# Output projections two tiles side by side, the pool mixer in fp32 ahead of the attention, gate chunks in the norms' tails

## The chip, the cores and the metric

The kernel runs on one core of a Trainium2 chip. A core has five engines with queues of their own: TensorE (PE, matmuls), VectorE (DVE), ScalarE (ACT), GpSimd (POOL) and SyncE (SP, which here issues the loads and stores). They work on SBUF, an on-chip memory of 128 partitions; PE writes to PSUM, 8 banks of 512 fp32 columns by 128 partitions. Each engine takes its instructions in order and waits on semaphores. The metric is the device time of one execution in microseconds.

## The reference

One inference step of a backbone of two layers over 1152 tokens (128 context tokens and 1024 latent tokens), width 1024, all in fp32:

```python
for l in range(DEPTH):                       # DEPTH = 2
    ada = silu(cond) @ w_ada[l] + b_ada[l]
    sh1, sc1, g1, sh2, sc2, g2 = split(ada, 6)
    u = layer_norm(x) * (1 + sc1) + sh1
    m = even_mixer(u) if l == 0 else odd_mixer(u)
    x = layer_norm(ALPHA * x + g1 * (m @ w_out[l]), ln_g[l, 0], ln_b[l, 0])
    u = layer_norm(x) * (1 + sc2) + sh2
    f = conv_ffn(u)                          # (silu(conv3(u @ w_up_a)) * (u @ w_up_g)) @ w_down
    x = layer_norm(ALPHA * x + g2 * f, ln_g[l, 1], ln_b[l, 1])

def even_mixer(u):    # layer 0
    q, k, v, p = split(u @ w_in)             # 512, 128, 128, 512 columns
    attn = attention(rope(rms(q)), rope(rms(k)), v)      # 8 heads, 2 key heads
    for g, w in enumerate((2, 4, 8, 16)):    # four groups of 128 columns
        pool[g] = (centred_mean(p[g], w) - p[g]) @ w_pool[g] * pool_scale[g]
    return concat(attn, pool)

def odd_mixer(u):     # layer 1
    h, b, c, f = split(u @ w_in)             # 768, 768, 768, 256 columns
    return concat(b * conv3(c * h), fourier(f))
```

`cond` is one vector for the latent and one for the context tokens; shifts, scales and gates follow from it. The new keys and values of the context are outputs too.

## The kernel before

The program is written out engine by engine; nothing schedules it, so the order of each engine's instructions is the order of its block of code, and semaphores tie the engines together.

**Products.** Nearly every fp32 product is made of three passes in fp32r, a reduced format: each operand is split into a rounded high part and the rest, the low part, and high*high, high*low and low*high are added in PSUM (`PASSES`). ACT rounds (`copy`, L812) and DVE subtracts (`lo`, L1272); of the weights of layer 0's output projection, four k-blocks are cast on DVE (L1502) and subtracted on POOL (`out_split`, L757). A few small products run in plain fp32: gates (L1795), columns for shift and scale (L1772, L1773, L1783), transposes (L1805).

**Tiles.** Tokens are taken as 9 tiles of 128 (the first is the context) or 3 chunks of 384. The contraction over 1024 columns is 8 k-blocks of 128. `act_a` and `act_b` hold activations transposed, k-block by k-block, high and low; the first four k-blocks of `act_b` are the attention's output, the last four the pool mixer's. In layer 1 the first six k-blocks of `act_a` are the conv mixer's and two the Fourier mixer's.

**Start.** SP issues the loads of constants, small parameters and bias rows, then w_ada in pieces of 512 KB into six slots. PE transposes the parameters into columns (L1741), ACT applies silu to the conditioning (L817), PE multiplies it with w_ada (L1751), and `top_cols` turns the first four blocks into columns: for two vectors and 8 k-blocks one matmul on the ada row (L1772) and one on the bias row (L1773), both in plain fp32.

**Layer 0.** POOL computes the pooled means in `pp`; PE, ACT and DVE make q, k and v. The attention goes over 18 groups (9 tiles x 2 key heads): `peak_scores` (L1937) and DVE's maxima (L1437), scores (L1958), exp on ACT (L1014), rounding on ACT, POOL's `p_low` (L749), the weighted sum (L1973, L1980), and DVE's division (L1442, L1448). When it is over, the pooled values are split into `ph` (ACT, DVE), mixed (L2033), scaled into `mf` on ACT (L1082) and split again into `act_b`, in turn with the weights `wo`.

**`ln_mid`.** In both layers it makes the output projection and the norms. `gates` expands three of four gate rows (g2 and g1, each for latent and context) over the partitions into banks 6 and 7, and ACT copies each. `project(tile)` makes 2 halves x 8 k-blocks x 3 passes = 48 matmuls of 512 columns into banks 2 x (tile mod 3) and the next. Then `ln_turn(tile)` (transposes of the second norm's output) alternates with `project(tile + 3)`, and in the tail with the three chunks of the first up unit of the feed-forward stage. The norm's chain for one tile is: DVE multiplies by the gate out of PSUM (L1324), adds alpha x (L1327) and takes statistics; ACT takes the root and normalises (L898); POOL applies gain and bias (L768, L770); DVE statistics again; ACT normalises into `ln_z` (L918); PE transposes (L1805); ACT modulates (L887) and rounds; DVE subtracts. `ln_act` and `ln_vec` run it in steps: in step s, ACT modulates tile s-2 first, then normalises tile s, then makes `ln_z` of tile s-1, and DVE takes up tile s, then s-1, then s-2. SP stores each normed tile, loads the next residual tile, and behind the last store issues the down weights' loads, the accumulator's loads (1.5 MB each) and the third up unit's.

**Feed-forward.** Eleven rounds in each layer, two up units and two gate units of 3 chunks in each, then the down projection (L2060) over 9 tiles, added up on DVE (L1556). A chunk is 24 matmuls (L1848).

## Time and profile before

| | us |
|---|---|
| runs, median (lowest to highest) | 3004.55 (3000.55 to 3005.01) |
| the profiled execution's own time | 3004.68 |
| its span, first to last instruction | 3002.9 |
| PE busy | 2771.1 |
| DVE busy | 1556.7 |
| ACT busy | 938.5 |
| POOL busy | 419.4 |

The profile is of one execution. Its times run from the span's start. The granted clock is the share of full speed that TensorE's clock had, 1.0 for 2.4 GHz and 0.5 for 1.2 GHz. In a timeline a row is one or several like instructions: start, duration, engine, line, tiles written and read, count, and in brackets the engine's idle time before it with what ended it. PEld is the weight load that goes with each matmul, SPq and ACTq are DMA issues. A plain fp32 matmul shows as two records.

### The profile page before, as it was taken

The page shows a single profiled execution, that of the slowest core. Times are in us where ns is not written, and L with a number is a line of the kernel's source. Part 1 is how long each engine was busy: PE and PEld are TensorE (multiplying, and loading weights), DVE is VectorE, ACT ScalarE, POOL GpSimd, SP SyncE. Part 2 cuts the span into 40 slices and gives each one's busy share as a digit, 9 for nine tenths or more (in the row PEclk, how much of TensorE's full clock was granted, in tenths as well). Part 3 has the DMA queues.
Part 4 walks back from the last instruction along what each step waited for, and adds up shares of the span by engine and source line. Part 5 has one row for each costly group of instructions (what it writes and reads, how often), then busy time and mean ns, then how long its engine had stood idle before and what let it go on. Part 6 is the DMA issues. An engine that isn't in the chain of part 4 may idle for free.

```text
span 3002.9 us, 36504 instructions
## 1 busy us (share of the span) xinstructions
PE 2771.1 (92%) x13992; PEld 2444.7 (81%) x13992; DVE 1556.7 (52%) x2166; ACT 938.5 (31%) x1417; POOL 419.4 (14%) x222
## 2 busy tenths in 40 slices
PE   6698699779899999999997899989899999999997
PEld 2387577648899999999993789968899999999996
DVE  0326688736555555555556333335655555555557
ACT  1611477635422222222224421124522222222223
POOL 0023377524000000000007000003200000000002
PEclk8799799979999999999998899989999999999999
DMA  7710100022311111111118131221311111111112
GB/s 288 265 46 7 42 1 1 0 77 86 134 43 42 42 42 42 42 42 42 42 36 288 56 103 38 69 85 64 145 40 40 42 42 42 42 42 42 42 35 77
DMA packets 172260, 202.26 MB, mean 67 GB/s; under 512 B 6843, under 2 KB 125207, under 8 KB 172179
## 3 DMA queue, kind: packets, MB, share of 16 engines
q1 hardware_dynamic: 171859, 200.83, 20.1%
q8 instruction: 54, 0.88, 0.1%
q10 hardware_dynamic: 320, 0.33, 0.0%
q14 instruction: 27, 0.22, 0.0%
HBM read 181.80 MB, written 19.33 MB: 67 GB/s over the span
## 4 chain that ended last, share of the span: by engine, by line
PE 79%; DVE 7%; ACT 5%; DMA 4%; POOL 3%; issue 2%; SPq 1%; ACTq 0%; POOLq 0%; DVEq 0%
PE ps L1848 47%; PE ps L2060 17%; PE ps L1826 7%; POOL p_low L749 2%; DVE small L1437 2%; DMA late_w<-in_w_ada 1%; DMA ada_w<-in_w_ada 1%; PE ps L1980 1%; PE ps L1795 1%; ACT p_top L812 1%; ACT p_exp L1014 1%; PE ps L1896 1%; ACT ln_u L887 1%; DMA raw_d<-in_k_pos 1%; PE ps L1937 1%
## 5 line engine op out<-in xcount | busy, mean ns | idle before, releaser
L1848 PE MATMUL ps<-act_b,uw 128*128 128x384 f32 x4608 | 822.2, 340 | 11.0 <-DVE act_b L1272 7.3
L1848 PEld LDWEIGHTS ps<-act_b,uw 128*128 128x128 f32 x4608 | 818.8, 189 | 12.9 <-DVE act_b L1272 7.9
L1848 PE MATMUL ps<-act_a,uw 128*128 128x384 f32 x3456 | 617.6, 340 | 5.3 <-DVE act_a L1272 5.3
L1848 PEld LDWEIGHTS ps<-act_a,uw 128*128 128x128 f32 x3456 | 614.5, 190 | 7.3 <-DVE act_a L1272 5.6
L2060 PE MATMUL ps<-dw,hh 128*128 128x512 f32 x2112 | 502.9, 397 | 8.7 <-DVE acc L1556 8.6
L2060 PEld LDWEIGHTS ps<-dw,hh 128*128 128x128 f32 x2112 | 398.1, 189 | 115.0 <-DVE acc L1556 10.4
L1556 DVE TENSOR_TENSOR acc<-acc,ps 128x512 f32<-128x512 f32 x360 | 246.8, 688 | 229.9 <-PE ps L2060 229.9
L812 ACT ACTIVATE fa<-ps 128x384 f32<-128x384 f32 (+2 forms) x176 | 67.5, 411 | 856.4 <-PE ps L1848 856.4
L1517 DVE TENSOR_SCALAR ft<-fa,fgrp 128x1153 f32<-128x1153 f32 x44 | 38.8, 883 | 309.9 <-ACT fa L812 309.9
L1272 DVE TENSOR_TENSOR uw<-raw_u,uw 128x1024 fp32r<-128x1024 f32 x112 | 136.7, 1222 | 117.5 <-ACT uw L812 113.8
L749 POOL TENSOR_TENSOR p_low<-p_exp,p_top 128x1536 fp32r<-128x1536 f32 (+1 forms) x50 | 170.9, 3418 | 92.1 <-ACT p_top L812 92.1
L1584 DVE TENSOR_TENSOR fh<-ft,ps 128x384 f32<-128x384 f32 (+2 forms) x176 | 75.2, 452 | 181.4 <-PE ps L1848 173.6
L812 ACT ACTIVATE uw<-raw_u 128x1024 fp32r<-128x1024 f32 x112 | 117.8, 1052 | 80.8 <-PE ps L1848 67.4
L794 POOL TENSOR_TENSOR acc<-acc,gb_end 128x1024 f32<-128x1024 f32 x9 | 21.4, 2378 | 835.3 <-ACT acc L1150 835.3
L812 ACT ACTIVATE hh<-fh 128x384 fp32r<-128x384 f32 x132 | 66.5, 520 | 218.7 <-DVE fh L1584 218.7
L787 POOL TENSOR_SCALAR acc<-acc,stats 128x1024 f32<-128x1024 f32 x9 | 10.8, 1202 | 832.7 <-DVE stats L1308 832.7
L1437 DVE TENSOR_REDUCE small<-ps 128x1 f32<-128x1152 f32 (+1 forms) x72 | 89.1, 1238 | 41.9 <-PE ps L1937 41.2
L768 POOL TENSOR_TENSOR ln_y<-ln_y,gbm 128x1024 f32<-128x1024 f32 x18 | 43.3, 2403 | 478.1 <-ACT ln_y L898 478.1
L1826 PE MATMUL ps<-wo,act_b 128*128 128x512 f32 x432 | 102.9, 399 | 0.0
L1826 PE MATMUL ps<-wo,act_a 128*128 128x512 f32 x432 | 102.3, 397 | 0.0
L887 ACT ACTIVATE ln_u<-ps,cols 128x128 f32<-128x128 f32 x216 | 78.4, 468 | 71.6 <-PE ps L1805 60.8
L1826 PEld LDWEIGHTS ps<-wo,act_b 128*128 128x128 f32 x432 | 82.6, 193 | 19.4 <-issue 2.3
(201 smaller groups left out, 3158.1 us busy)
## 6 DMA issues: line engine op xcount, KB each, us to landing
raw_u<-in_w_up SPq DMA_DIRECT2D x88, 512.0 KB, 3.7
ada_w<-in_w_ada SPq DMA_DIRECT2D x64, 512.0 KB, 6.4
raw_d<-in_w_down SPq DMA_DIRECT2D x44, 512.0 KB, 3.5
late_w<-in_w_ada SPq DMA_DIRECT2D x32, 512.0 KB, 6.0
raw_u<-in_w_in_odd SPq DMA_DIRECT2D x20, 512.0 KB, 3.6
ln_y<-in_x_all SPq DMA_DIRECT2D x18, 512.0 KB, 4.3
xs<-ln_y SPq DMA_DIRECT2D x18, 512.0 KB, 2.6
acc<-xs SPq DMA_DIRECT2D x6, 1536.0 KB, 11.5
```

What stands on the lines that cost most here:

```text
L749: gp.tensor_tensor(p_low[:, s % 3, 0:nb, :], p_exp[:, s % 2, 0:nb, :], p_top[:, s % 3, 0:nb, :].bitcast(F32), ALU.subtract).then_inc(p_lo, 1)
L768: gp.tensor_tensor(y, y, gb[:, 0, :], ALU.mult).then_inc(g_mul, 1)
L812: return act.activation(o, i, ACT.Copy)
L887: o = act.activation(ln_u[:, k * P:(k + 1) * P], ps[:, 6 + k // 4, (k % 4) * P:(k % 4 + 1) * P], ACT.Identity, bias=cols[:, l, c0, k, cc:c ...
L1272: return v.tensor_tensor(dst, src, hi.bitcast(F32), ALU.subtract)
L1437: v.tensor_reduce(g.peak(h), ps[:, 0:nb, 0:nw], mybir.AxisListType.XY, ALU.max, negate=True).then_inc(mx_done, 1)
L1517: chain(v.tensor_scalar(dst[:, 1:1 + n], line[:, 0:n], w(0), w(3), ALU.mult, ALU.add))
L1556: return v.tensor_tensor(a, a, ps[:, 6 + j % 2, :], ALU.add).then_inc(down_added, 1)
L1584: o = v.tensor_tensor(f_h[l][:, s0:s0 + ln], f_t[l][:, p0:p0 + ln], ps[:, 3 + c, s0 - c * CH:s0 - c * CH + ln], ALU.mult)
L1826: mm = pe.matmul(ps[:, 2 * (tile % 3) + h, :], src[:, k, a, tile * P:(tile + 1) * P], wo[l][:, k, w, 512 * h:512 * (h + 1)], start=(k, a, ...
L1848: mm = pe.matmul(out, uw[:, u_slot, w, k, :], src[:, k, a, c * CH:(c + 1) * CH], start=(k, w, a) == (0, 0, 0), stop=(k, w, a) == (KD - 1, ...
L2060: mm = pe.matmul(ps[:, 6 + h, :], hh[l][:, b, a, tile * P:(tile + 1) * P], w_[:, b, w, 512 * h:512 * (h + 1)], start=(b, a, w) == (0, 0, 0 ...
```

## The change

**Start.** The constants and eight of the small loads move from SP's queue to ACT's; SP issues three small loads (conditioning, context conditioning, and the first 2048 values of `b_ada` as 16 more rows of the matrix that is transposed anyway) ahead of w_ada. The bias thereby becomes 16 columns of `par`. `top_cols` has one matmul for each k-block, and DVE adds the bias when it copies the columns out (`cols_of`).

**Pool mixer.** w_pool stays fp32, `ph` and its splitting go. Twelve pieces of 384 tokens are multiplied in plain fp32: three ahead of the last keys' transpose, one ahead of the first peak scores, eight between the four peak scores of group 0. ACT scales them into `mixed`. They are split behind the attention.

**Splitting of `wo` in layer 0.** ACT rounds all eight k-blocks, DVE subtracts all eight; `out_split` on POOL is gone. The order is 7, 6, 2, 3, 5, 4, 0, 1, and the splits of `mixed` and those of the last attention group stand among them. SP loads gate rows, residual tiles and gains earlier.

**`ln_mid`.** Tiles 0 and 1 are projected side by side, the contraction outermost, so that each k-block waits only for itself; the four gates stand between k-blocks, g1 first. The other projections run one tile further ahead of the transposes. In the tail, chunks of the first up unit and of the first gate unit alternate, and both units are split before the norms.

```diff
             def top_cols():
-                pe.wait_ge(b_top, 32)
                 pe.wait_ge(ada_bank, 3 + ADA_TOP)
                 for n in range(2):
                     for k in range(KD):
-                        out = ps[:, 6 + n, 2 * k:2 * k + 2]
-                        pe.matmul(out, ada_top[:, 2 * n + k // 4, (k % 4) * P:(k % 4 + 1) * P], con[:, C_FOLD:C_FOLD + 2], start=True, stop=False)
-                        mm = pe.matmul(out, bias_row[n][0:1, k * P:(k + 1) * P], con[0:1, C_SELB:C_SELB + 1].broadcast_to([1, 2]), start=False, stop=True)
+                        mm = pe.matmul(ps[:, 6 + n, 2 * k:2 * k + 2], ada_top[:, 2 * n + k // 4, (k % 4) * P:(k % 4 + 1) * P],
+                                       con[:, C_FOLD:C_FOLD + 2], start=True, stop=True)
...
+            def mix(m):
+                g, c = divmod(m, NCH)
+                bank = MIX_BANKS[m % 3]
+                if m == 0:
+                    pe.wait_ge(pool_done, 1)
+                    pe.wait_ge(wp_ld, 16)
+                    pe.wait_ge(qkv_free, NT - 1)
+                if m >= 3:
+                    pe.wait_ge(mix_ev, m - 2)
+                for u0, ln, p0 in PPIECES[c]:
+                    mm = pe.matmul(ps[:, bank, u0 - c * CH:u0 - c * CH + ln], wp[:, g, :], pp[:, g, p0:p0 + ln], start=True, stop=True)
+                mm.then_inc(mix_done, 1)
...
             turn_queries(0)
+            mix(3)
             for h in range(G):
                 peak_scores(0, h)
+                mix(4 + 2 * h)
+                mix(5 + 2 * h)
...
-                gates(l)
-                project(0)
-                pe.wait_ge(gate_rdy, 4 * l + 3)
-                gate(0, ln_u)
-                project(1)
-                project(2)
-                pe.wait_ge(gate_rdy, 4 * l + 4)
-                for tile in range(NT):
-                    ln_turn(tile, i4)
-                    if tile + 3 < NT:
-                        project(tile + 3)
-                    if tile >= NT - 3:
-                        first_chunk(tile - (NT - 3))
+                gate_after = {2: 1, 4: 2, 5: 3, 6: 4} if l == 0 else {-1: 1, 4: 2, 5: 3, 6: 4}
+                def side_by_side():
+                    if -1 in gate_after:
+                        mid_gate(l, gate_after[-1])
+                    for n, k in enumerate(OUT_ORDER):
+                        ready(k)
+                        for tile in range(SIDE):
+                            for h in range(2):
+                                for a, w in PASSES:
+                                    mm = pe.matmul(ps[:, 2 * tile + h, :], src[:, k, a, tile * P:(tile + 1) * P], wo[l][:, k, w, 512 * h:512 * (h + 1)],
+                                                   start=n == 0 and (a, w) == (0, 0), stop=n == KD - 1 and (a, w) == (1, 0))
+                            if n == KD - 1:
+                                mm.then_inc(out_done, 1)
+                        if n in gate_after:
+                            mid_gate(l, gate_after[n])
+                side_by_side()
+                for tile in range(SIDE, 4):
+                    project(tile)
+                pe.wait_ge(gate_rdy, 4 * l + 4)
+                for tile in range(5):
+                    ln_turn(tile, i4)
+                    project(tile + 4)
+                for tile, c, gate_unit in ((5, 0, 0), (6, 0, 1), (7, 1, 0), (8, 1, 1)):
+                    ln_turn(tile, i4)
+                    first_chunk(gate_unit, c)
+                first_chunk(0, 2)
+                first_chunk(1, 2)
```

The order of PE's instructions in layer 0, from the attention's end to the first transposes of the norms, before (L2033 the mixer, L1795 gates, L1826 projections, L1805 transposes):

```order
L1980 MATMUL ps<-p_low,vv 128x512 x3
L2033 MATMUL ps<-ph,wp 128x384 x36
L1795 MATMUL ps<-ln_z,con 128x512 x4
L1795 MATMUL ps<-ln_u,con 128x512 x2
L1826 MATMUL ps<-wo_110,act_b 128x512 x48
L1795 MATMUL ps<-ln_u,con 128x512 x2
L1826 MATMUL ps<-wo_110,act_b 128x512 x96
L1805 MATMUL ps<-con,ln_z 128x128 x8
```

and now (L1864 the two tiles side by side, L1816 gates, L1879 single tiles, L1826 transposes):

```order
L2053 MATMUL ps<-p_low,vv 128x512 x3
L1864 MATMUL ps<-wo_112,act_b 128x512 x36
L1816 MATMUL ps<-ln_u,con 128x512 x2
L1864 MATMUL ps<-wo_112,act_b 128x512 x24
L1816 MATMUL ps<-ln_u,con 128x512 x2
L1864 MATMUL ps<-wo_112,act_b 128x512 x12
L1816 MATMUL ps<-ln_z,con 128x512 x2
L1864 MATMUL ps<-wo_112,act_b 128x512 x12
L1816 MATMUL ps<-ln_z,con 128x512 x2
L1864 MATMUL ps<-wo_112,act_b 128x512 x12
L1879 MATMUL ps<-wo_112,act_b 128x512 x96
L1826 MATMUL ps<-con,ln_z 128x128 x8
```

The mixer has left this place, the first gate stands behind three k-blocks, and two more single tiles come before the first transposes.

PE at the tail of layer 0's norms, before (the last projection, then transposes and chunks of the up projection):

```order
L1826 MATMUL ps<-wo_110,act_b 128x512 x48
L1805 MATMUL ps<-con,ln_z 128x128 x8
L1848 MATMUL ps<-act_b,uw 128x384 x24
L1805 MATMUL ps<-con,ln_z 128x128 x8
L1848 MATMUL ps<-act_b,uw 128x384 x24
L1805 MATMUL ps<-con,ln_z 128x128 x8
L1848 MATMUL ps<-act_b,uw 128x384 x240
```

and now:

```order
L1879 MATMUL ps<-wo_112,act_b 128x512 x48
L1826 MATMUL ps<-con,ln_z 128x128 x8
L1905 MATMUL ps<-act_b,uw 128x384 x24
L1826 MATMUL ps<-con,ln_z 128x128 x8
L1905 MATMUL ps<-act_b,uw 128x384 x24
L1826 MATMUL ps<-con,ln_z 128x128 x8
L1905 MATMUL ps<-act_b,uw 128x384 x24
L1826 MATMUL ps<-con,ln_z 128x128 x8
L1905 MATMUL ps<-act_b,uw 128x384 x216
```

Four transposes instead of three stand behind the last projection, and three chunks among them instead of two.

DVE behind the attention of layer 0, now (`mixed` is the mixer's output, `wo` from `raw_d` k-blocks 7, 6, 0, 1 and from `out_raw` 2, 3, 5, 4):

```order
L1293 TENSOR_TENSOR act_b<-mixed_100,act_b 128x1152
L1293 TENSOR_TENSOR wo_112<-raw_d,wo_112 128x1024
L1293 TENSOR_TENSOR act_b<-mixed_99,act_b 128x1152
L1293 TENSOR_TENSOR wo_112<-raw_d,wo_112 128x1024
L1467 RECIPROCAL o_inv<-o_raw 64x128 x4
L1473 TENSOR_TENSOR o_f<-ps,o_inv 64x256 x2
L1293 TENSOR_TENSOR wo_112<-out_raw_110,wo_112 128x1024
L1293 TENSOR_TENSOR act_b<-o_f,act_b 128x2x128
L1293 TENSOR_TENSOR wo_112<-out_raw_110,wo_112 128x1024
L1293 TENSOR_TENSOR act_b<-mixed_98,act_b 128x1152
```

Before, the last group's division came first, and all of the splitting behind it.

## Rows read from the trace of the kernel before

**Rows 1.** The page: busy time of each engine over the span:

```profile
PE 2771.1 (92%) x13992; PEld 2444.7 (81%) x13992; DVE 1556.7 (52%) x2166; ACT 938.5 (31%) x1417; POOL 419.4 (14%) x222
```

**Rows 2.** Windows: length, busy us of each engine, granted clock, DMA share:

```profile
625.00:650.00 25.00, 22.77 (x55) 13.04 (x54) 0.28 (x1) 3.07 (x3) 0.00 (x0) 0.63 0.05 20
...
2000.00:2025.00 25.00, 14.93 (x21) 6.42 (x22) 7.34 (x7) 7.94 (x9) 0.00 (x0) 0.50 0.42 150
```

**Rows 3.** Timeline of PE, layer 0: start us, us, what, [idle before]:

```profile
586.31 0.97 PE L1980 MATMUL ps<-p_low,vv 128*128 128x512 f32 x3 [1.89 <-POOL p_low L749]
...
624.07 3.77 PE L1795 MATMUL ps<-ln_z,con 9*128 9x512 f32 x4 [16.08 <-DVE wo L1272]
...
637.55 13.96 PE L1826 MATMUL ps<-wo,act_b 128*128 128x512 f32 x48
651.45 1.98 PE L1795 MATMUL ps<-ln_u,con 9*128 9x512 f32 x4
653.35 22.06 PE L1826 MATMUL ps<-wo,act_b 128*128 128x512 f32 x96
```

**Rows 4.** Timeline of PE, layer 1: gate rows and first projections:

```profile
2007.84 3.75 PE L1795 MATMUL ps<-ln_z,con 9*128 9x512 f32 x4 [11.90 <-DMA ln_u<-in_b_ada]
...
2021.29 13.33 PE L1826 MATMUL ps<-wo,act_a 128*128 128x512 f32 x48
...
2036.46 15.71 PE L1826 MATMUL ps<-wo,act_a 128*128 128x512 f32 x68
```

**Rows 5.** Timeline of all engines, start of the program:

```profile
5.08 13.50 SPq L454 DMA_DIRECT2D ada_w<-in_w_ada  x12
...
10.33 1.94 PE L1751 MATMUL ps<-ada_w,conds 128*32 128x512 f32 x8 [3.95 <-DMA ada_w<-in_w_ada]
...
36.07 0.56 PE L1772 MATMUL ps<-con,ada_top 128*128 128x2 f32 x2 [0.80 <-ACT ada_top L812]
...
52.06 0.58 PE L1773 MATMUL ps<-con,bias_row 1*128 1x2 f32 x2
...
52.91 4.50 PE L1751 MATMUL ps<-ada_w,conds 128*32 128x512 f32 x24 [0.27 <-DVE cols L1291]
```

**Rows 6.** Timeline of PE, from the last keys to the first peaks:

```profile
311.38 0.69 PE L1905 MATMUL ps<-con,k 128*128 128x128 f32 x2 [8.39 <-DVE k L1272]
...
315.87 0.47 PE L1937 MATMUL ps<-kt,q_top 128*128 128x128 f32 x1 [2.11 <-DVE q_low L1272]
...
319.31 1.11 PE L1945 MATMUL ps<-con,small 128*128 128x128 f32 x4 [0.39 <-DVE small L1437]
```

**Rows 7.** Timelines of POOL, DVE and ACT, end of the attention:

```profile
582.79 3.46 POOL L749 TENSOR_TENSOR p_low<-p_exp,p_top 128x1536 fp32r<-128x1536 f32 x1 [1.85 <-ACT p_top L812]
...
583.05 3.48 DVE L1272 TENSOR_TENSOR act_b<-o_f,act_b 128x256 fp32r<-128x256 f32 x1 [4.46 <-ACT act_b L812]
587.94 3.38 DVE L1442 RECIPROCAL o_inv<-o_raw 64x128 f32<-64x128 f32 x4 [1.41 <-ACT o_raw L812]
...
592.70 0.43 DVE L1272 TENSOR_TENSOR act_b<-o_f,act_b 128x256 fp32r<-128x256 f32 x1 [0.48 <-ACT act_b L812]
...
597.82 1.04 ACT L812 ACTIVATE wo<-raw_d 128x1024 fp32r<-128x1024 f32 x1
...
603.77 1.22 DVE L1272 TENSOR_TENSOR wo<-raw_d,wo 128x1024 fp32r<-128x1024 f32 x1
```

**Rows 8.** Timelines of PE and ACT, end of the norms in layer 0:

```profile
745.94 1.03 PE L1805 MATMUL ps<-con,ln_z 128*128 128x128 f32 x8
...
754.98 1.09 PE L1805 MATMUL ps<-con,ln_z 128*128 128x128 f32 x8 [3.78 <-ACT ln_z L918]
...
762.14 1.09 PE L1805 MATMUL ps<-con,ln_z 128*128 128x128 f32 x8 [0.30 <-ACT ln_z L918]
768.58 31.75 PE L1848 MATMUL ps<-act_b,uw 128*128 128x384 f32 x167 [5.34 <-DVE act_b L1272]
...
778.96 1.06 ACT L812 ACTIVATE uw<-raw_u 128x1024 fp32r<-128x1024 f32 x1 [3.27 <-DMA raw_u<-in_w_up]
```

More of the change, by code:

```diff
@@ L76 @@
 D_DOWN1 = D_OUT1 + 4
-OUT_EXTRA = range(2, 6)
+OUT_RAW = (7, 6, 0, 1)
+OUT_EXTRA = (2, 3, 5, 4)
+OUT_ORDER = (7, 6, 2, 3, 5, 4, 0, 1)
+SIDE = 2
+MIX_BANKS = (6, 7, 3)
 END_BANKS = (0, 2, 0, 2, 0, 6, 4, 6, 4)
@@ L230, in build @@
         q_lat = at("q_lat", [P, NQ, AW], F32, off_b + 36864 + 18816)
+        mixed = [at(f"mixed{g}", [P, TOK], F32, off_b + 36864 + 4704 * (g - 1) if g else off_q + 11776) for g in range(NPG)]
         p_exp = at("p_exp", [P, 2, TRI, G * P], F32, off_a)
@@ L890, in step @@
                     if i1 is not None and s.live(0):
-                        if s.first(0):
-                            gate(4)
                         st = stats[:, s.slot(0), :]
@@ L1034, in o_round, with mix_out, wo_hi, mixed_hi @@
                 copy(act_b[:, 2 * g.kv:2 * g.kv + 2, 0, g.token * P:(g.token + 1) * P], o_f[:]).then_inc(m_hi, 1)
+            def mix_out(m):
+                g, c = divmod(m, NCH)
+                act.wait_ge(mix_done, m + 1)
+                act.activation(mixed[g][:, c * CH:(c + 1) * CH], ps[:, MIX_BANKS[m % 3], 0:CH], ACT.Identity,
+                               bias=0.0, scale=par[:, 200 + g:201 + g]).then_inc(mix_ev, 1)
+            def wo_hi(l, k, d0):
+                if k in OUT_EXTRA:
+                    act.wait_ge(out_ld, 64 * (l + 1))
+                    copy(wo[l][:, k, 0, :], out_raw[l][:, OUT_EXTRA.index(k), :]).then_inc(out_hi, 1)
+                    return
+                n = d0 + OUT_RAW.index(k)
+                d_hi_at(n % 2, n // 2 + 1, wo[l][:, k, 0, :])
+            def mixed_hi(g):
+                if g == NPG - 1:
+                    act.wait_ge(mix_ev, NPG * NCH)
+                    act.wait_ge(q_dup, NGR)
+                elif g < 2:
+                    act.wait_ge(mix_lo, NPG - 1 - g)
+                copy(act_b[:, 4 + g, 0, :], mixed[g][:]).then_inc(mix_hi, 1)
+            for m in range(3):
+                mix_out(m)
             act.wait_ge(qkv_free, NT)
             q_round(0)
+            for m in range(3, NPG * NCH):
+                mix_out(m)
             peaks(0)
@@ L1177, in _ @@
             f.hi_u(0, 0)
+            f.hi_u(0, 1)
             ln_act("mid0", act_b)
@@ L1236, in _ @@
                         copy(act_a[:, bass.ds(b, 1), 0, c * CH:(c + 1) * CH].rearrange("p a n -> p (a n)"), c_m[:, c * CH:(c + 1) * CH]).then_inc(cm_hi, 1)
-            for k in range(KD):
+            for k in OUT_ORDER:
                 wo_hi(1, k, D_OUT1)
+            f = Ffn(1, U_FFN1, D_DOWN1)
+            f.hi_u(0, 1)
             ln_act("mid1", act_a)
-            Ffn(1, U_FFN1, D_DOWN1).run()
+            f.run()
             act.wait_ge(gb_ld, 32 * 4)
@@ L1566, in body @@
                             self.gated(g, 1)
-                        self.lo_u(g, 2 * b + 1)
+                        lead = b == 0 and isinstance(g, int) and g == 0
+                        if not lead:
+                            self.lo_u(g, 2 * b + 1)
                         if b == 1:
@@ L2066, in ffn_group @@
                     for gate_unit in range(2):
-                        if first and b == 0 and gate_unit == 0:
+                        if first and b == 0:
                             continue
```

290 lines of the change are left out of this document (142 added, 148 removed).

## The prediction

> **What bounds the kernel now.** I read the page first. TensorE (PE) is busy 92% of the span [rows 1], so little can be had where it runs and something only where it waits or runs at its lower clock. I then laid windows over the program and looked for stretches with a low granted clock or a busy share below full: 0.63 at 625 to 650 us although PE is busy 22.8 of 25 us, and 0.50 at 2000 to 2025 us [rows 2]. 0.5 is 1.2 GHz and 1.0 is 2.4 GHz, so both stretches ran (nearly) all at the lower level. The timeline of PE names the places.
>
> Layer 0: the attention's last matmuls end at 586.31 + 0.97 = 587.3. Mixer, weight splitting and three gate matmuls follow, and the first projection begins at 637.55, 50 us later [rows 3]. Tile 0 takes 13.96 us, tiles 1 and 2 together 22.06, so a tile costs 11.03 at the full clock, and tile 1 ends at 653.35 + 11.03 = 664.4. From the attention's end to tile 1's end is 77.1 us. Two tiles and four gates at the full clock are only 22.1 + 4 x 1.98 = 30.0.
>
> Layer 1: the conv stage ends at 2007.84 - 11.90 = 1995.9; PE waits 11.90 us for the gate rows' DMA, tile 1 ends at 2036.46 + 11.03 = 2047.5 [rows 4]. That is 51.6 us for the same 30.0.
>
> Start: 36.07 to 52.64 is one run of 32 tiny matmuls, and the load queue's PE consumer comes next, at 52.91 [rows 5]. End of the norms: PE idles 3.78, 0.30 and 5.34 us between transposes and up projection [rows 8].
>
> **The change part by part.**
>
> *Bias columns.* 16 of the 32 matmuls go. (52.64 - 36.07) / 32 = 0.52 us each, so 8.3 us. They are on the path: DVE's first column and the next ada matmuls wait for them [rows 5], and the slots for w_ada are full by then, so the loads resume as much earlier. SP's first w_ada load is issued at 5.08 behind twelve small issues [rows 5]; now three stand ahead, some 3 us less. But PE needs the conditioning first, whose parameters now come by ACT's queue, and six slots are all that can be filled before PE releases some. PE's first block is at 10.33. I bound this from +0.4 to -2.5 and take -1.3. Together -9.6.
>
> The Trainium skill, "DMA: Bandwidth & Descriptors", section "Queues, rings and completion order", says each DMA engine serves the queues round-robin, packet by packet; the small parameter loads would then share the engines with 512 KB loads rather than go first. By that rule the order of the issues gains nothing (2950 in place of 2949). No row here shows two queues loading at the start.
>
> *Mixer in fp32 ahead of attention.* Twelve pieces of 384 columns. The nearest fp32 row is the gate: its two products of 512 columns (four records) take 3.77 us at the low clock and 1.98 at the high one [rows 3], so a 384 piece is 1.41 or 0.74. Three run in the 8.39 us for which PE waits for the last keys [rows 6]: free. One runs in the 2.11 us before the first peak: nearly free. Eight stand between the four peak scores of group 0, each of which waits for a DVE maximum anyway. 315.87 to 319.31 are 3.4 us now. All at the low clock they would be 8 x 1.41 + 4 x 0.47 = 13.2 (9.8 more), all at the high one, with the peaks at half their time, 6.9 (3.5 more, less 0.7 because the transposes behind them run faster). PE came back to the high clock inside tile 0's 48 matmuls, when nothing interrupted them [rows 3]; I take the change in the middle of the eight, 4.5 us. Bounds +2.8 and +9.8.
>
> *Layer 0, attention's end to tile 1.* Now ACT rounds and DVE subtracts: mixed 3, weights 7, mixed 2, weights 6, then the last group's inverse and scaling, then 2, 3, 5, 4, 0, 1. A rounding on ACT is 1.04, a subtraction on DVE 1.22 [rows 7] (1.37 for 1152 columns, by width). DVE's subtraction of group 16 begins at 583.05 and takes 3.48 where the same one later takes 0.43: it ends as POOL's p_low of 582.79 + 3.46 does [rows 7]. So DVE is free at 586.5; mixed 3 and weights 7 are ready at 589.1, weights 6 at 591.7. Then 3.38 + 0.87 (reciprocals, scaling); weights 2 at 597.1, 3 at 599.1, 5 at 601.7, 4 at 604.5, 0 and 1 by 606.9. ACT keeps ahead and comes to the gates' copies at 606.9, the first done at 607.9.
>
> A k-block is 12 matmuls, 2.76 us. PE: 7 and 6 from 589.1 to 594.6; waits 2.5; k = 2 to 599.9; gate 1 to 601.8; 3 and 5 to 607.4; waits 0.6 for ACT's copy; gate 2, k = 4, gate 3, k = 0, gate 4, k = 1 end at 622.3. That is 35.0 us after the attention. If the clock drops in the two waits, some k-blocks run at half speed, up to 3 us more; I add 1.5: 36.5 against 77.1, -40.6. All of this is also the price if the cover fails: what is late next is DVE, in steps of 1.22, not PE.
>
> The Trainium skill, "SBUF — State Buffer", section "SBUF: two separate sides", calls the port pair of DVE and GpSimd an exclusive lock held for a whole instruction. The 3.48 against 0.43 agrees. Were it not so, weights 7 would be ready at 587.3 and the sum 1.8 us lower.
>
> *Layer 1.* Gate rows are asked for in the last conv block, so gate 1 runs at 1996 to 1998 while PE is still at 2.4 GHz. Eight subtractions of 1.22 follow the last of the conv: weights 7 ready at 1999.4, 6 at 2000.5, and from there PE is slower (2.76) than DVE, so only the first is waited for. ACT copies gate 1 at 2008.4 behind eight roundings and one for the up weights; gate 2 isn't due before 2013. PE: 1999.4 + 22.1 + three gates 5.9 = 2027.4, plus 0.4 for the clock: 2027.8 against 2047.5, -19.7.
>
> *The tails of the norms.* Projections run one tile further ahead: the transpose of tile t now stands behind projection t + 3, before behind t + 2. But ACT's step s first modulates tile s - 2, so it waits for that transpose before it normalises tile s. The norm chain starts each tile one projection later. Call T the end of projection 8. Before: transposes of 6, 7, 8 at T, T + 9.0, T + 16.2, and the last activation at T + 22.6 [rows 8]. After: 5, 6, 7, 8 at T, + 9.0, + 19.1 (a full step again, plus 1.1 because DVE takes up tile 8 only when it has done with 5), + 26.3; last activation + 32.8. Four chunks of up projection (31.75 / 167 x 24 = 4.56 us [rows 8]) lie in that instead of two. What is left afterwards is two chunks instead of four: T + 32.8 + 9.1 = 41.9 against T + 22.6 + 18.2 = 40.8. The pairing buys back what the lag costs. Then a new wait: the third up unit's load, queued by SP behind the last norm's store and the accumulator's loads, landed at 778.96 = T + 33.0 [rows 8], before its need at T + 40.8. It follows the last tile's normalising, which is 10 us later, so it lands at T + 43, and with ACT's rounding and DVE's subtraction the unit is ready at 45.5. So the next unit starts 4.7 later than before; a transpose less before T gives 0.8 back, the clock takes 1. +4.9 for each layer, +9.8 for both. Bounds per layer: -6.1 (the lag costs nothing) and +9 (all filler chunks at 1.2 GHz).
>
> *Sum:* -9.6 + 4.5 - 40.6 - 19.7 + 9.8 = -55.6. The profiled execution took 3004.68 (span 3002.9 and 1.8 around it), 0.13 above the median of the runs: 3004.7 - 55.6 = 2949.
>
> **Rivals.**
> 1. *The lag in the norms is not there* (ACT gets ahead, or the steps overlap): 11 us less in each layer, 2927. For it: DVE and ACT are far from full. Against: the instruction order makes ACT wait for the transpose.
> 2. *The clock stays low in the broken-up stretches*: mixer +5, first k-blocks +2, filler chunks 4 in each layer, 2964. For it: rows 2, where 91% busy hardly raised it.
> 3. *The start gains nothing*, because w_ada's loads set the pace and the matmuls only filled their wait: 2959. Against: PE's wait before 52.91 is for DVE, and 24 matmuls run there without waiting for a load.
> 4. *Slower:* both side-by-side stages, 30.0 us each at the high clock, run wholly at 1.2 GHz because gates and waits stand between the k-blocks: +60, 3009. It decides from 55.6 us of extra time on, so both layers have to stay low to the last k-block. For it: gates and waits kept 0.63 [rows 2]. Against: here runs of 12 full matmuls stand between the gates, and PE comes into both stages at the high clock, after waits of 1.8 us and nothing; there it came from waits of 16 and 12 us [rows 3, 4].
>
> **How the numbers follow.** Forecast 0.52; rival 1 0.13, rival 2 0.18, rival 3 0.10, rival 4 0.02; 0.05 for a gain that is smaller for a reason I don't see. The forecast's own range is 2938 to 2960. For 8 in 10 I take 2932 to 2966, which holds rivals 2 and 3 and leaves out 1 and 4. A change under 0.2%, 6 us, can't be told from none. Faster 0.96, within 0.2% 0.01, slower 0.03.
>
> **What would show it.** 16 tiny matmuls ending near 42 us. The first peaks' transposes 4 to 5 us later relative to the keys. First projection 2 us behind the attention's last matmul, tile 1's end 36 us behind it, with 1.0 as the clock; in layer 1 31 to 32 us behind the conv. In the tails four transposes behind projection 8, 9 to 10 us apart, and a wait of ACT or PE for the third up unit's load. I am wrong if that wait is missing, if the fp32 pieces take over 1 us on average, or if PE waits for more than 4 us in a side-by-side stage.

## The result, and the profile after

The changed kernel takes 2928.2 us (median of 4 runs, 2926.3 to 2931.4) against 3004.3 beside it: a ratio of 0.975 with a 95% interval of 0.9733 to 0.9767, 76 us less. 2949 was predicted, with a range of 2932 to 2966: the sign was right, but the time came out 21 us below the forecast and outside the range. The profiled execution took 2926.9, its span is 2925.1 (before: 3002.9).

PE's line on the page [rows 1]:

```profile
PE 2726.4 (93%) x13956; PEld 2408.8 (82%) x13956; DVE 1558.3 (53%) x2157; ACT 935.4 (32%) x1420; POOL 410.2 (14%) x218
```

The low window of layer 0 is gone [rows 2]. Windows of the changed kernel (length, busy us of each engine, granted clock, DMA share, GB/s):

```profile
600.00:625.00 25.00, 25.00 (x96) 17.14 (x95) 11.50 (x17) 7.81 (x9) 2.46 (x1) 1.00 0.00 0
625.00:650.00 25.00, 25.00 (x116) 20.79 (x115) 12.93 (x27) 9.80 (x17) 12.67 (x6) 1.00 0.21 72
```

Timeline of PE, layer 0, from the attention's end to tile 2 [rows 3]:

```profile
584.39 7.36 PE L1864 MATMUL ps<-wo,act_b 128*128 128x512 f32 x24 [1.73 <-DVE wo L1293]
...
614.53 3.02 PE L1864 MATMUL ps<-wo,act_b 128*128 128x512 f32 x12
617.39 21.93 PE L1879 MATMUL ps<-wo,act_b 128*128 128x512 f32 x96
```

The attention ends at 582.66; the first projection begins 1.73 us behind it (before: 50), and tile 1 is done at 617.4. Behind the first wait 24 matmuls take 7.36 in place of 5.5: the granted clock of 584 to 592 us is 0.79, so it was low for a while. From 592 us on it is 1.00.

Layer 1 [rows 4]:

```profile
1936.55 1.98 PE L1816 MATMUL ps<-ln_u,con 9*128 9x512 f32 x4
1940.12 15.27 PE L1864 MATMUL ps<-wo,act_a 128*128 128x512 f32 x60 [1.59 <-DVE wo L1293]
...
1969.81 21.93 PE L1879 MATMUL ps<-wo,act_a 128*128 128x512 f32 x96
```

The end of the norms in layer 0 [rows 8]. T, the end of projection 8 (the last tile's), is 698.09 here:

```profile
698.09 1.03 PE L1826 MATMUL ps<-con,ln_z 128*128 128x128 f32 x8
...
706.65 1.24 PE L1826 MATMUL ps<-con,ln_z 128*128 128x128 f32 x8 [3.37 <-ACT ln_z L927]
...
717.15 1.49 PE L1826 MATMUL ps<-con,ln_z 128*128 128x128 f32 x8 [3.66 <-ACT ln_z L927]
...
724.30 1.09 PE L1826 MATMUL ps<-con,ln_z 128*128 128x128 f32 x8 [0.30 <-ACT ln_z L927]
...
730.74 8.59 PE L1905 MATMUL ps<-act_b,uw 128*128 128x384 f32 x48 [1.18 <-DVE act_b L1293]
744.01 27.25 PE L1905 MATMUL ps<-act_b,uw 128*128 128x384 f32 x144 [4.68 <-DVE uw L1293]
```

The last four transposes stand at T, + 8.6, + 19.1 and + 26.2, and the third unit begins at T + 45.9, behind a new wait of 4.68 for uw. The prediction had 0, 9.0, 19.1, 26.3 and 45.5.

The start [rows 5]: the parameters' transposes wait until 9.68, the first ada block comes at 12.53 (before 10.33), and from the start of the run of 32 records (16 matmuls) to the next ada matmul it is 7.25 us (before 16.8). That run ends at 45.7, where the prediction had 42.

```profile
9.68 0.90 PE L1764 MATMUL ps<-con,prow 88*128 88x88 f32 x4 [9.68 <-DMA prow<-in_pool_scale]
12.53 5.35 PE L1774 MATMUL ps<-ada_w,conds 128*32 128x512 f32 x24 [1.95 <-ACT conds L826]
...
38.72 6.99 PE L1793 MATMUL ps<-con,ada_top 128*128 128x2 f32 x32 [0.71 <-ACT ada_top L814]
45.97 4.10 PE L1774 MATMUL ps<-ada_w,conds 128*32 128x512 f32 x24 [0.27 <-DVE cols L1314]
```

And a place the prediction had left out: a feed-forward round of layer 0, whose code is unchanged. The kernel before, then the changed one:

```profile
1065.53 50.85 PE L1848 MATMUL ps<-act_b,uw 128*128 128x384 f32 x288
1116.22 2.94 PE L2060 MATMUL ps<-dw_ctx,hh 128*128 128x512 f32 x12
```

```profile
1096.76 50.09 PE L1905 MATMUL ps<-act_b,uw 128*128 128x384 f32 x288
1146.69 2.96 PE L2120 MATMUL ps<-dw_ctx,hh 128*128 128x512 f32 x12
```

From start to start, 288 matmuls take 50.69 us before and 49.93 after: 176.0 and 173.4 ns each, at a granted clock of 1.0 in both. Below, this time from the start of one matmul to the start of the next is called the pitch. The program has 8064 matmuls of this form (4608 + 3456 on the page). At 2.6 ns each that would be 21 us; the page's busy time for them falls by 17.0 us (from 822.2 + 617.6 to 812.0 + 610.8).

Where the time went, by PE's timeline (spans of the profiled executions; the parts sum to the whole difference):

| stretch | before | after | difference | predicted |
|---|---|---|---|---|
| start to the last keys' transpose | 311.4 | 303.8 | -7.6 | -9.6 |
| to the attention's end (mixer) | 275.9 | 278.9 | +3.0 | +4.5 |
| to tile 1, layer 0 | 77.1 | 34.7 | -42.4 | -40.6 |
| to the first down products, layer 0 | 148.6 | 153.7 | +5.1 | +4.9 |
| 10 rounds of layer 0 | 758.5 | 751.2 | -7.3 | 0 |
| to the conv's end | 424.4 | 414.3 | -10.2 | 0 |
| to tile 1, layer 1 | 51.6 | 33.3 | -18.3 | -19.7 |
| to the first down products, layer 1 | 148.2 | 155.5 | +7.4 | +4.9 |
| 10 rounds of layer 1 | 758.6 | 751.2 | -7.4 | 0 |
| rest | 48.6 | 48.6 | 0 | 0 |
| sum | 3002.9 | 2925.1 | -77.8 | -55.6 |

The rows with a forecast sum to -52.8 against -55.6. The miss lies in three rows that were set to zero: they sum to -24.9.

### The profile page after: what moved, and what is told of

The parts are those of the page before. It is cut to its first block, busy times and chain, and to the rows that moved or that the text cites. A ratio compares the mean times of both kernels' runs of the same rounds, so it can differ in the third digit from the quotient of the medians.

```text
span 2925.1 us, 36419 instructions
## 1 busy us (share of the span) xinstructions
PE 2726.4 (93%) x13956; PEld 2408.8 (82%) x13956; DVE 1558.3 (53%) x2157; ACT 935.4 (32%) x1420; POOL 410.2 (14%) x218
## 4 chain that ended last, share of the span: by engine, by line
PE 79%; DVE 6%; DMA 5%; ACT 5%; POOL 3%; issue 2%; SPq 1%; ACTq 0%; POOLq 0%; DVEq 0%
PE ps L1905 46%; PE ps L2120 18%; PE ps L1879 5%; POOL p_low L758 2%; DMA late_w<-in_w_ada 2%; PE ps L1864 1%; DVE small L1462 1%; DMA ada_w<-in_w_ada 1%; DMA raw_u<-in_w_up 1%; PE ps L2053 1%; ACT p_exp L1020 1%; PE ps L1953 1%; ACT p_top L814 1%; ACT ln_u L898 1%; DMA raw_d<-in_k_pos 1%
## 5 line engine op out<-in xcount | busy, mean ns | idle before, releaser
L1905 PE MATMUL ps<-act_b,uw 128*128 128x384 f32 x4608 | 812.0, 339 | 11.6 <-DVE uw L1293 4.7
L1905 PEld LDWEIGHTS ps<-act_b,uw 128*128 128x128 f32 x4608 | 807.7, 190 | 13.9 <-DVE uw L1293 5.0
L1905 PE MATMUL ps<-act_a,uw 128*128 128x384 f32 x3456 | 610.8, 339 | 6.9 <-DVE uw L1293 5.7
L1905 PEld LDWEIGHTS ps<-act_a,uw 128*128 128x128 f32 x3456 | 606.5, 190 | 10.5 <-DVE uw L1293 6.1
L1145 ACT ACTIVATE ft<-ft 128x1153 f32<-128x1153 f32 x44 | 51.6, 1172 | 129.7 <-DVE ft L1538 123.7
L1020 ACT ACTIVATE p_exp<-ps 128x1536 f32<-128x1536 f32 (+1 forms) x50 | 71.1, 1422 | 62.2 <-PE ps L2032 62.2
L1293 DVE TENSOR_TENSOR dw<-raw_d,dw 128x1024 fp32r<-128x1024 f32 (+1 forms) x61 | 73.7, 1208 | 27.9 <-ACT dw L814 27.9
```

The costliest lines, as they stand in the source:

```text
L1020: act.activation(p_exp[:, s % 2, 0:nb, :], ps[:, 3:3 + nb, :], ACT.Exp).then_inc(exp_done, 1)
L1145: act.activation(ft[:, 1:PADW - 2], ft[:, 1:PADW - 2], ACT.Silu).then_inc(silu_done, 1)
L1293: return v.tensor_tensor(dst, src, hi.bitcast(F32), ALU.subtract)
L1905: mm = pe.matmul(out, uw[:, u_slot, w, k, :], src[:, k, a, c * CH:(c + 1) * CH], start=(k, w, a) == (0, 0, 0), stop=(k, w, a) == (KD - 1, ...
```

## Experiments: the matmuls that nobody changed

The one thing that the change does to those matmuls is to grow `par` from 220 to 236 columns. Tiles are placed one behind the other in steps of 32 bytes, so all that follows `par`, the weights `uw` and `dw` among it, moves by 64 bytes. The activations (`act_a`, `act_b`, `hh`) lie ahead of it and stay. Below, *distance* is the address of uw (or dw) less that of the activations, modulo 256 bytes, from the program's own layout: 128 before, 192 after.

**64 and 32 bytes in the kernel before.** The other kernel has `end[0] += 32` at the same place.

```diff
         par = fixed("par", [P, 220])
+        end[0] += 64
         conds = fixed("conds", [P, 48])
```

> The kernel before with 64 bytes left free behind the parameter columns, so that the raw weights, the split up-projection weights (uw) and all behind them lie 64 bytes further on, as in the changed kernel; nothing else is touched. Theory A (the address sets the pitch of the up projection's matmuls): a feed-forward round takes 75.12 us in place of 75.88, the page's group for the up matmuls 1423 us in place of 1440, and the time falls by 15 us (20 rounds) plus 4 for the conv stage, to 2983 to 2987. Theory B (the shorter rounds come from where the changed program's instructions lie, or from its queues): rounds stay at 75.88, 3004. Theory C (the chip's day): rounds of the kernel before itself differ between runs, and this one stays within 3 us of it.

> The kernel before with 32 bytes left free at the same place. Theory A with a step of 64 bytes (what counts is whether a weight row begins on a 64-byte border): the matmuls differ from both known cases, and rounds may be longer than 75.88. Theory A with any shift off the 512-byte border: 75.12, some 2985. Theory B or C: 75.88, 3004.

Measured: 2982.4 us for 64 bytes (2980.8 to 2988.2, ratio 0.9935, 0.9918 to 0.9951) and 3013.1 for 32 (ratio 1.0032, 1.0019 to 1.0044), before 3003.4. Timelines of PE with 64 and with 32:

```profile
1063.26 50.09 PE L1849 MATMUL ps<-act_b,uw 128*128 128x384 f32 x288
1113.19 2.96 PE L2061 MATMUL ps<-dw_ctx,hh 128*128 128x512 f32 x12
```

```profile
1070.76 51.04 PE L1849 MATMUL ps<-act_b,uw 128*128 128x384 f32 x288
1124.44 22.65 PE L2061 MATMUL ps<-dw,hh 128*128 128x512 f32 x96
```

49.93 from start to start again, in the kernel before: theory A. 32 bytes (distance 160) make it slower than either (51.04 and 22.65).

**Which tile.** One kernel has the 64 bytes ahead of uw, the other behind it, where `off_s` begins:

```diff
+        end[0] += 64
         off_uw = end[0]
...
         uw = fixed("uw", [P, 2, 2, KD, P], F32R)
+        end[0] += 64
         off_s = end[0]
```

> The kernel before with 64 bytes left free behind uw, so that only the region of the norm rows, keys, values and down weights (dw) is shifted, and uw stays where it was. If uw's own address counts for the up projection (theory A), up chunks stay at 50.85 us for 288 matmuls and rounds at 75.88, within 3 us of 3004; the down matmuls could change, whose weights are shifted here (22.5 us for 96 in a round). If the distance between other buffers counts, rounds fall to 75.12 and the time to 2985.

> The kernel before with 64 bytes left free directly in front of uw: the raw weights, the statistics and the parameter columns keep their places, uw and what lies behind it (dw among it) move by 64 bytes. Theory A1 (the address of uw alone, the stationary operand of the up projection): 288 up matmuls take 50.1 us as in the changed kernel, rounds 75.12, some 2983. Theory A2 (the raw weights, from which ACT and VectorE fill uw during the matmuls, or the small tiles): 50.85, 75.88, 3004.

Measured: behind uw 3000.3 (ratio 0.9996, 0.9987 to 1.0006), ahead of it 2986.0 (ratio 0.9949, 0.9932 to 0.9967). Timeline of PE, the kernel with 64 bytes ahead of uw:

```profile
1060.66 50.09 PE L1849 MATMUL ps<-act_b,uw 128*128 128x384 f32 x288
```

With the 64 bytes behind uw, 288 up matmuls stay at 50.86. The raw weights, the small tiles and dw have no part in it. It is uw.

**Its address, or its distance.**

```diff
-        base = (nc.sbuf_base + 31) // 32 * 32
+        base = (nc.sbuf_base + 31) // 32 * 32 + 64
```

> The kernel before with every tile 64 bytes further on, the activations too. Theory R (what counts is the distance of uw from the activations, the moving operand): 50.85 us for 288 up matmuls, 3004 as before. Theory S (the border on which uw itself begins counts): 50.1, 2983 to 2987.

Measured: 3003.8 (ratio 1.0012, 1.0002 to 1.0022).

```profile
1066.46 50.85 PE L1848 MATMUL ps<-act_b,uw 128*128 128x384 f32 x288
```

uw begins where it does in the changed kernel, modulo 256, and is as slow as before, since the activations moved along: theory R.

**The changed kernel at other distances.** `end[0] += 64` behind `par` (distance 0), and `+= 192` (distance 128, as in the kernel before).

> The changed kernel with 64 bytes more left free behind the parameter columns, so that the weights lie 128 bytes further on than in the kernel before (64 bytes further than in the changed kernel). Theory A with a period of 128 bytes: the rounds go back to 75.88 and the time to 2947 to 2950, which is the sum as it was predicted. Theory A with a longer period (256 or 512): rounds stay at 75.12, 2928. Theory B: 75.12, 2928.

> The changed kernel with 192 bytes more left free behind the parameter columns: 256 in all against the kernel before, the distance at which the matmuls are as slow as there. Nothing else differs from the changed kernel. Theory (the addresses alone made the time come out below the sum of the prediction): rounds 75.88, 2948 to 2951. Rival (something else in the change made the rounds shorter, and the addresses only happen to do the same): 2928 to 2935.

Measured: 2917.6 (2915.3 to 2918.6) at distance 0, where I had expected a repeat every 128 bytes or no change; and 2945.1 (2941.3 to 2949.7, ratio 0.9808, 0.9791 to 0.9825) at distance 128. Timelines of PE, distance 0 and distance 128:

```profile
1072.37 21.96 PE L2121 MATMUL ps<-dw,hh 128*128 128x512 f32 x96
1094.17 50.11 PE L1906 MATMUL ps<-act_b,uw 128*128 128x384 f32 x288
```

```profile
1075.72 22.56 PE L2121 MATMUL ps<-dw,hh 128*128 128x512 f32 x96
1098.12 50.85 PE L1906 MATMUL ps<-act_b,uw 128*128 128x384 f32 x288
```

At distance 0 the down matmuls are faster too, 21.96 for 96 in place of 22.56. At the distance of the kernel before, the changed kernel takes 17 us more than at its own (2928.2), and 4 us less than the 2949 of the prediction.

**PE alone.** Behind the last down matmul of the changed kernel PE goes on with blocks such as this, the uw side shifted by `o` and the activations by `m` columns of 4 bytes:

```diff
+            for n_, w_, x_ in ups(8, 0): pe.matmul(ps[:, n_, 0:CH], w_, x_, start=True, stop=True)
+            for n_, w_, x_ in downs(8, 0): pe.matmul(ps[:, n_, :], w_, x_, start=True, stop=True)
```

> The changed kernel, after whose last down matmul PE goes on with matmuls whose products nobody reads, while VectorE and ACT finish the last norms and then stand idle. Thirteen blocks of 126 matmuls in the form of the up projection (stationary 128 columns of uw, moving 384 of the activations) and twelve of 192 in the form of the down projection (stationary 128 columns of the activations, moving 512 of uw), each block with its operands shifted by so many bytes: the uw side by 0 to 224 in steps of 32 (0 here is 64 bytes behind the kernel before), then the uw side by 0, 64, 128, 192 with the activations 64 bytes further on. Theory R (two operand streams of PE alone, by their distance modulo 256): blocks differ with nobody else at work, 173.9 ns a matmul at the good distances against 176.5 at the bad one (up form) and 228.6 against 235 (down form), and moving both sides by 64 gives the same as moving neither. Theory K (PE loses time against what ACT, VectorE and the DMAs read and write): with them idle all blocks of a form take the same time, to 0.2%.

In the windows from 2940 us on, DVE, ACT and POOL are busy for 0.00 us, and the clock is 1.00. Timeline of PE: `ups` with o = 0, 8, 16, 24, 32, 40, 48, 56 (L2260 to L2267), `ups` with m = 16 and o = 48 (L2272), `downs` with o = 0, 8, 16 and 24 (L2273 to L2276), and `downs` with m = 16 and o = 32 (L2283):

```profile
2935.48 22.01 PE L2260 MATMUL ps<-act_a,uw 128*128 128x384 f32 x126
2957.32 22.42 PE L2261 MATMUL ps<-act_a,uw 128*128 128x384 f32 x126
2979.58 22.00 PE L2262 MATMUL ps<-act_a,uw 128*128 128x384 f32 x126
3001.42 22.01 PE L2263 MATMUL ps<-act_a,uw 128*128 128x384 f32 x126
3023.27 22.17 PE L2264 MATMUL ps<-act_a,uw 128*128 128x384 f32 x126
3045.27 22.42 PE L2265 MATMUL ps<-act_a,uw 128*128 128x384 f32 x126
3067.53 22.34 PE L2266 MATMUL ps<-act_a,uw 128*128 128x384 f32 x126
3089.70 22.42 PE L2267 MATMUL ps<-act_a,uw 128*128 128x384 f32 x126
...
3199.68 22.42 PE L2272 MATMUL ps<-act_a,uw 128*128 128x384 f32 x126
3221.94 22.57 PE L2273 MATMUL ps<-uw,act_a 128*128 128x512 f32 x96
3244.34 22.55 PE L2274 MATMUL ps<-uw,act_a 128*128 128x512 f32 x96
3266.73 21.93 PE L2275 MATMUL ps<-uw,act_a 128*128 128x512 f32 x96
3288.50 22.57 PE L2276 MATMUL ps<-uw,act_a 128*128 128x512 f32 x96
...
3444.97 21.94 PE L2283 MATMUL ps<-uw,act_a 128*128 128x512 f32 x96
```

Start to start, per matmul, by distance (192 + 4 x o, modulo 256):

| distance | 0 | 32 | 64 | 96 | 128 | 160 | 192 | 224 |
|---|---|---|---|---|---|---|---|---|
| up form, ns | 173.3 | 173.4 | 174.6 | 176.7 | 176.0 | 176.7 | 173.3 | 176.7 |
| down form, ns | 226.8 | 233.3 | 229.0 | 233.5 | 233.2 | 234.3 | 233.3 | 233.2 |

Theory R: nobody else is at work, and the 173.3 ns at distance 192 and the 176.0 at 128 are what the two kernels show. With both sides moved by 64 bytes, seven of eight blocks are as by their distance; one is not (L2272, up form, distance 64: 22.26 us from start to start in place of 22.00 for L2264), so the distance alone isn't the whole rule. The blocks of the down form have 96 matmuls, not 192 as announced. Distance 160, which no other exceeds in either form here, was the slowest in the kernel too (32 bytes).

The Trainium skill, "SBUF — State Buffer", section "Who interferes with whom", says that PE never waits on anyone. The run agrees as far as the other engines go: with them idle the pitches are those of the busy kernels (173.3 for 173.4, 176.0 for 176.0). What it shows besides is a loss that comes with the place of PE's own operands: 2% between the best and the worst distance with 384 columns moving, 3% with 512.

## Experiments: the changed stages

**Side by side undone.** Tiles 0 and 1 one after the other, contraction inside; order of weights, gates, mixer unchanged.

```diff
-                    for n, k in enumerate(OUT_ORDER):
-                        ready(k)
-                        for tile in range(SIDE):
-                            for h in range(2):
+                    for tile in range(SIDE):
+                        for h in range(2):
+                            for n, k in enumerate(OUT_ORDER):
```

> The changed kernel with tiles 0 and 1 projected one after the other (half by half, contraction inside), the order of the weights, the gates and everything else kept. Theory (side by side, the first k-blocks of both tiles fill the time in which ACT and VectorE prepare the next weights): tile 0's first half goes at the pace of the weights and the gate rows, ends at 608 to 610, then come 5.5 and 11.0 us, so that tile 1 ends at 625 to 627 in layer 0 in place of 617.4 (8 to 9 us more, and up to 5 more if the clock is low behind the waits), and 1 to 4 us more in layer 1: 2938 to 2944. Rival (most of the gain came from the order of the weights and the moved mixer, PE would have had to wait no more than 3 us): 2928 to 2932.

Measured: 2958.1 (2954.1 to 2960.4), 30 us more than the changed kernel. Timeline of PE in this kernel:

```profile
591.05 1.65 PE L1865 MATMUL ps<-wo,act_b 128*128 128x512 f32 x3 [3.92 <-DVE wo L1293]
592.63 3.78 PE L1816 MATMUL ps<-ln_u,con 9*128 9x512 f32 x4
...
614.90 20.04 PE L1865 MATMUL ps<-wo,act_b 128*128 128x512 f32 x75
634.78 21.93 PE L1879 MATMUL ps<-wo,act_b 128*128 128x512 f32 x96
```

A window of the same kernel:

```profile
600.00:620.00 20.00, 19.37 (x30) 9.17 (x31) 2.00 (x2) 4.93 (x5) 0.00 (x0) 0.50 0.00 1
```

Tile 1 ends 53.4 us behind the attention (34.7 side by side), and in layer 1 44.9 behind the conv (33.3). My 8 to 9 us, 13 or 14 with a low clock, were too few. PE's waits are 7.9 us in layer 0 (2.3 side by side) and 4.8 in layer 1 (1.6), 8.8 more in all. The stages are 30.3 longer; the other 21 us go with the clock: a gate takes 3.78 in place of 1.98, three matmuls 1.65 (12 side by side 3.02), and with PE busy for 19.37 of 20 us the granted clock is 0.50, 1.2 GHz, where the changed kernel has 2.4 GHz from 592 us on. Side by side is worth 30 of the 61 us gained in both stages.

**Loads earlier.** The small loads back ahead of w_ada on SP's queue, and in both layers the third up unit's load issued ahead of the norms' loads:

```diff
             mid_gains(0)
+            f.u(0, 2)
             ln_loads("mid0", t["x_all"], xs[0])
```

> The changed kernel with two orders of DMA issues altered. (1) The small parameter loads go back to SP's queue, ahead of the first w_ada loads, as in the kernel before; the two b_ada rows stay. (2) In both layers the third up unit's load is issued before the norms' loads and stores, not behind them. Theory: (1) the first ada block starts at 10.3 in place of 12.5 and the column matmuls at 36 in place of 38.7: 2.2 to 2.7 us less; (2) PE's waits for uw of 4.7 and 5.7 us behind the first six chunks go: together 12 to 13 us, 2915 to 2916. Rival to (1): the six slots of w_ada are late either way, and nothing is gained. Rival to (2): the load was late only by the profile's reckoning, VectorE's taps stand ahead of the split, and 2 to 3 us of each wait stay: 2920.

Measured: 2917.0 (2915.9 to 2918.7), some 11 us less; the profiled spans differ by 8.2. Timeline of PE:

```profile
5.97 0.91 PE L1771 MATMUL ps<-con,prow 88*128 88x88 f32 x4 [5.97 <-DMA prow<-in_b_ada]
10.11 1.94 PE L1781 MATMUL ps<-ada_w,conds 128*32 128x512 f32 x8 [3.23 <-DMA ada_w<-in_w_ada]
...
741.41 25.24 PE L1912 MATMUL ps<-act_b,uw 128*128 128x384 f32 x144 [1.45 <-DVE uw L1300]
```

(1) The first ada block comes at 10.11 in place of 12.53, but the attention ends at 583.3 against 582.7: the gain is gone by then. Over all runs the first q product starts at 205.6 to 209.1 in six kernels with the old start, at 198.6 to 200.4 in five with ACT's queue and at 195.9 to 200.8 in five with SP's; a difference of 1 us can't be told here. (2) T is 698.71 and the unit begins at T + 42.7 in place of 45.9, in layer 1 at T + 42.8 in place of 47.1: 7.5 us. 1.45 us of the wait stay. ACT has the unit rounded at 737.28, but DVE stands in three taps of the convolution from 736.43 on and begins its subtraction only at 740.14. That is what the rival named, VectorE's taps ahead of the split; it had 2 to 3 us staying.

**The lag taken back.** In addition, transposes of tiles 0 to 5 stand inside the projections, three or four quarters of a tile apart, and that of tile 6 behind projection 8.

```diff
+                            if k in (3, 7) and 4 * (tile - SIDE) + 2 * h + (k + 1) // 4 in TURN_AT:
+                                ln_turn(TURN_AT.index(4 * (tile - SIDE) + 2 * h + (k + 1) // 4), i4)
```

> As the run before it, and the lag of one projection in the norms taken back: the transposes of tiles 0 to 5 stand inside the projections, behind quarters 6, 10, 13, 17, 20 and 24 counted from tile 2's start (4 quarters to a tile), so that the transpose of tile 6 stands behind projection 8 again, with two chunks after it, one between 7 and 8 and three at the end. The norm's chain needs 8.8 us from one transpose to the next, three quarters and a transpose are 9.0. Theory (the lag costs what the prediction says, last activation at T + 32.8 against T + 22.6): the next unit starts at T + 32.5 to 34 in place of T + 45.9 in the changed kernel, some 8 us per layer less than in the run before this one, 2899 to 2901. Rival: transposes between the matmuls of a projection make PE wait for the chain in each tile (1 us in each of five), and the gain is eaten up: 2910 to 2916.

Measured: 2895.8 (2892.8 to 2899.7, ratio 0.9652, 0.9635 to 0.9669), 21 us less than the run before it. 19.9 of them are the two tails. Timeline of PE from T on:

```profile
693.53 1.04 PE L1834 MATMUL ps<-con,ln_z 128*128 128x128 f32 x8
...
709.87 1.09 PE L1834 MATMUL ps<-con,ln_z 128*128 128x128 f32 x8 [1.94 <-ACT ln_z L935]
...
726.34 25.24 PE L1918 MATMUL ps<-act_b,uw 128*128 128x384 f32 x144 [1.45 <-DVE uw L1301]
```

No transpose within the projections is waited for, and the unit begins at T + 32.8 in both layers, 9.9 and 10.0 earlier.

**The distance chosen.** That kernel at distances 0, 64 and 128 (192 above): `end[0] += 64`, `128` or `192` behind `par`.

> The kernel of the run 'turns moved into the projections' with 64 bytes more left free behind the parameter columns (128 bytes in all against the kernel before). Theory (distance to the activations counts, for uw and for dw each by itself): 288 up matmuls 50.1 us, 96 down matmuls 21.95 in place of 22.56, rounds 74.5; 20 rounds save 12 us: 2883 to 2885, the fastest version of the study. If it is not a matter of distance but of the changed kernel's program, no such gain: 2896.

> The same with 192 bytes in all. If the effect repeats every 128 bytes, up 50.1 and down 22.56 as at 64 bytes (rounds 75.1, 2896). If every distance that is no multiple below 128 is as good as 128 bytes (a threshold), up 50.1 and down 21.95 (rounds 74.5, 2884).

> The same with 256 bytes in all. If it repeats every 256 bytes, this is the slow case again: up 50.85 and down 22.55, rounds 75.88, 2911. If every 128 bytes, or with a threshold, up 50.1 and down 21.95, 2884. If every 512 bytes, in between.

Measured: 2883.5 (2880.8 to 2885.8, ratio 0.9606, 0.9593 to 0.9619) at distance 0, 2900.9 at 64 and 2915.2 at 128; at 192 it was 2895.8. The values at 64 and at 128 are medians of two runs each. At 128 a round is 75.89 as in the kernel before, whose weights lie 256 bytes nearer. At 64 the down matmuls take 22.14, between the others, but the up matmuls have no one pitch. Timeline of PE, two rounds of that kernel:

```profile
856.44 51.04 PE L1919 MATMUL ps<-act_b,uw 128*128 128x384 f32 x288
...
932.04 50.09 PE L1919 MATMUL ps<-act_b,uw 128*128 128x384 f32 x288
```

From start to start the 288 take 50.88 and 49.93 (176.7 and 173.4 ns), in other rounds 50.3, and a whole round takes 74.65 to 75.62. The odd block of PE alone was at this distance too. Distance 0 is the fastest version of the study, 45 us below the changed kernel.

## Why the prediction was wrong

- **The step that failed** is a term that the sum puts at nothing, without a reason: what the growth of `par` does to the matmuls outside the changed stages. The prediction priced the 16 new columns by what they save at the start. But they moved uw by 64 bytes, and each of the up matmuls became 2.6 ns shorter: 14.7 us in the twenty rounds of the table and 3.8 in the conv stage. Whole runs put it at 14 to 21: -21.0 for the kernel before with 64 bytes behind `par`, -14 with 64 ahead of uw, and 17 lost by the changed kernel when it is put back to the old distance (2945.1, inside the stated range). The signs of being wrong that the prediction named did not come up (the new wait is there, eight fp32 pieces take 7.8 us, PE waits 2.3 and 1.6 us): all of them watch the changed stages.
- **To the conv's end, -10.2.** 1440 matmuls x 2.6 ns are 3.8 us of it. The other 6 lie where the late w_ada loads come in; from the last down products of layer 0 to the next up chunk it took 78.9 to 82.6 us in six runs with that stage as before (82.1 in the profile predicted from) and 75.8 to 79.3 in ten with it as after (75.8 in the one compared). Which part of that is the change's stays open.
- **Attention's end to tile 1: right in the main, but the clock's cost and the second wait overlap.** 34.7 against 36.5. The clock did fall in the first wait, and 24 matmuls took 1.9 us longer. But that ran into the second wait, which shrank from the 2.5 forecast to 0.61, so the 1.5 added for the clock was not needed, nor the 0.6 for ACT's copy. Layer 1: 33.3 against 31.9; the four gates run one by one at 1.98 as said, and behind the first wait 60 matmuls take 15.27 where 13.8 were counted (granted clock 0.93 from 1941 to 1956 us).
- **Bias columns: the matmuls right, the order of issues wrong.** The 32 tiny matmuls became 16 (16.8 to 7.25 us). But the first ada block came 2.2 us later, where 1.3 us of gain was taken and 0.4 of loss was the bound. On ACT's queue the last small load (`pool_scale`) was issued at 3.75 us and the parameters were there at 9.68, with SP's w_ada loads under way from 1.91; on SP's queue it was issued at 4.16 and they were there at 5.50 (at 5.97 with that order restored). The Trainium skill, "DMA: Bandwidth & Descriptors", "Queues, rings and completion order", says that each DMA engine serves the queues round-robin, packet by packet. The trace agrees: not the issue was late but the landing. How much of the 4 us is this sharing and how much ACT's queue itself isn't told apart.
- **Mixer:** +3.0 for +4.5. The prediction put the rise of the clock in the middle of the eight pieces, but its own prices then give 10.0 us in place of 3.4, 6 more after the 0.7 for the transposes, not 4.5. Measured from the first peak to the transposes behind the last it is 7.6 (307.62 to 315.25) in place of 3.4. The four pairs take 2.87, 1.93, 1.51 and 1.50 us: the clock rose in the second pair, earlier than assumed. That 4.5 came close is in part luck.
- **Tails:** the lag, its spacing and the new wait were where they had been put. Taking the lag back gave 9.9 and 10.0 us and the wait 3.2 and 4.3. The term was +9.8 and came out at +12.5; it was low in layer 1, where the unit begins at T + 47.1. The 4.56 us of a chunk was read from a row whose first part ran at the low clock (0.50 from 768 to 772 us of the kernel before); at the high clock a chunk is 4.2. The wait for the load covered that.
- **The rivals.** Rival 1 (no lag, 2927) names the time that was measured, and is false: the transposes stand at the lag's spacing. Rival 2's low clock came in part: in the first k-blocks (7.36 for 5.5 and 15.27 for 13.8), and in two of the four filler chunks of each tail, which take 5.94 and 5.71, 5.29 and 5.15 where one at the high clock takes 4.41 (0.76 at 706 to 713 and at 717 to 724 us). That is 4.5 us in the tails, for the 8 that it named. Rival 3's start did gain, 7.6. Rival 4's mechanism, a clock that stays low where gates and waits break up the matmuls, does exist, as the run with three matmuls between gates and waits shows; side by side it doesn't hold.

## What to carry to other kernels

A change that adds or widens a tile moves every tile behind it: before a gain or loss is put down to the edit, compare the durations of matmuls that weren't touched, and try a few paddings of 32 or 64 bytes on a kernel bound by PE: 32 bytes cost 10 us here and 64 gave 21. Name signs of being wrong for the stretches that should not change, too. Where a stage waits for operands piece by piece, put a second tile's work behind each piece: it fills the waits, and here it kept PE at 2.4 GHz between the gates. When projections run further ahead, let the transposes keep their spacing inside them, or the tail pays a full step.
